# Eight pieces instead of one or two for a table sent to HBM, and three waits moved by some columns, in a one-core 512-token kernel

## What is computed

```python
def chunk(xc):                                   # 128 tokens
    s = ...                                      # scores of 8 heads against 2 x 128 sub-keys
    top_s, top_i = lax.top_k(s, PEER_TOPK)
    cand_s = top_s[:, :, 0, :, None] + top_s[:, :, 1, None, :]
    cand_i = top_i[:, :, 0, :, None] * PEER_N_KEYS + top_i[:, :, 1, None, :]
    ...
    best_s, best_pos = lax.top_k(cand_s, PEER_TOPK)
    idx = jnp.take_along_axis(cand_i, best_pos, axis=-1)
    g = jax.nn.softmax(best_s, axis=-1)
    u = jnp.take(expert_u, idx, axis=0)
    v = jnp.take(expert_v, idx, axis=0)
    act = jax.nn.gelu(jnp.einsum('td,thkd->thk', xc, u))
    return jnp.einsum('thk,thkd->td', (g * act).astype(v.dtype), v)
```

## Time and profile before

| | before |
|---|---|
| median of 3 runs | 3500.95 us (3498.36 to 3501.43) |
| profiled execution | 3489.53 us, its span 3487.6 us |
| mean granted TensorE clock | 0.959 |
| TensorE busy | 3200.6 us, 92% of the span |
| VectorE / ScalarE / GpSimd busy | 1991.2 / 1329.8 / 1312.2 us |
| moved by DMA | 636.86 MB, mean 183 GB/s |

### The profile page before, as it was taken

The page is one execution under the profiler, slowest core; times in us unless marked ns, Lnnn a source line. Parts: engine busy times, 40 slices in busy tenths (PEclk is TensorE's granted clock), DMA queues, the critical chain, the costliest instruction groups (busy, mean ns, idle before and its releaser), DMA issues.

```text
span 3487.6 us, 44563 instructions
## 1 busy us (share of the span) xinstructions
PE 3200.6 (92%) x15088; PEld 2733.2 (78%) x15088; DVE 1991.2 (57%) x2967; ACT 1329.8 (38%) x1959; POOL 1312.2 (38%) x654
## 2 busy tenths in 40 slices
PE   4999779998999989999968778999989897999999
PEld 3888658886888778788856657899979897888887
DVE  6552375512553154411047676878768675788887
ACT  3222232223322232322234553244849482333333
POOL 3444334443444444344423203365433333222321
PEclk9999879999999999999989889999999898999999
DMA  5554325532554222222312103254798989999997
GB/s 225 193 192 145 102 89 194 193 109 73 201 194 141 97 79 97 87 97 98 99 52 69 49 19 103 91 167 155 241 340 252 339 290 386 321 367 359 364 361 275
DMA packets 234647, 636.86 MB, mean 183 GB/s; under 512 B 22560, under 2 KB 104736, under 8 KB 233504
## 3 DMA queue, kind: packets, MB, share of 16 engines
q1 hardware_dynamic: 87408, 318.49, 26.8%
q10 hardware_dynamic: 110256, 182.59, 14.7%
q0 software_dynamic: 36864, 134.23, 10.7%
HBM read 580.69 MB, written 54.53 MB: 182 GB/s over the span
## 4 chain that ended last, share of the span: by engine, by line
issue 39%; PE 36%; POOL 17%; DMA 4%; DVE 3%; ACT 1%; POOLq 0%; ACTq 0%; DVEq 0%
POOL wlo L473 17%; PE bank L1854 5%; PE bank L1856 5%; PE bank L1855 5%; PE bank L1524 5%; PE bank L1525 5%; PE bank L1526 5%; DMA ring<-u_rows_dram,cell_u 4%; PE bank L1815 3%; DVE ring L1373 1%; PE bank L1721 1%; POOL ring L492 0%; DVE wlo L1361 0%; DVE rstd L966 0%; DVE sp L1279 0%
## 5 line engine op out<-in xcount | busy, mean ns | idle before, releaser
L473 POOL TENSOR_TENSOR wlo<-raw,whi 128x1024 fp32r<-128x1024 f32 x394 | 999.7, 2539 | 1458.2 <-ACT whi L511 1457.9
L1524 PE MATMUL bank<-hhi,whi 128*128 128x512 f32 (+1 forms) x2832 | 1062.4, 375 | 60.2 <-DVE wlo L1361 28.8
L1525 PE MATMUL bank<-hlo,whi 128*128 128x512 f32 (+1 forms) x2832 | 1052.6, 372 | 0.0
L1526 PE MATMUL bank<-hhi,wlo 128*128 128x512 f32 (+1 forms) x2832 | 1052.3, 372 | 0.0
L511 ACT ACTIVATE whi<-raw 128x1024 fp32r<-128x1024 f32 x599 | 633.7, 1059 | 1010.4 <-PE bank L1526 618.3
L1524 PEld LDWEIGHTS bank<-hhi,whi 128*128 128x128 f32 x2832 | 537.7, 190 | 136.3 <-DVE wlo L1361 29.7
L1525 PEld LDWEIGHTS bank<-hlo,whi 128*128 128x128 f32 x2832 | 537.3, 190 | 71.6 <-issue 1.4
L1526 PEld LDWEIGHTS bank<-hhi,wlo 128*128 128x128 f32 x2832 | 536.4, 189 | 71.8
L927 DVE CUSTOM_DVE_ANT_0 ada_raw<-ada_raw,cond_row 128x1024 f32<-128x1024 f32 x128 | 307.5, 2433 | 152.0 <-DMA ada_raw<-ada_dram 152.0
L1361 DVE TENSOR_TENSOR wlo<-raw,whi 128x1024 fp32r<-128x1024 f32 x205 | 250.7, 1223 | 115.5 <-ACT whi L511 93.0
L1854 PE MATMUL bank<-whi,we 128*128 128x512 f32 x768 | 299.8, 390 | 14.6 <-ACT act_out L804 14.6
(11 more groups left out here) (244 smaller groups left out, 3682.2 us busy)
## 6 DMA issues: line engine op xcount, KB each, us to landing
raw<-stream_dram SPq DMA_DIRECT2D x599, 512.0 KB
ada_raw<-ada_dram ACTq DMA_DIRECT2D x128, 512.0 KB, 4.0
expert_acts<-act_out ACTq DMA_DIRECT2D x128, 192.0 KB
g_ring<-expert_weights ACTq DMA_DIRECT2D x128, 192.0 KB
act_in<-expert_acts ACTq DMA_DIRECT2D x128, 192.0 KB
first_raw<-ada_dram ACTq DMA_DIRECT2D x8, 1024.0 KB, 23.2
expert_weights<-spread ACTq DMA_DIRECT2D x2, 4096.0 KB, 25.0
x<-xin_dram SPq DMA_DIRECT2D x1, 2048.0 KB, 12.0
```

The costliest lines, as they stand in the source:

```text
L473: pool.tensor_tensor(wlo[:, s, :, :], raw[:, s, :, :], whi[:, s, :, :].bitcast(F32), ALU.subtract).then_inc(lo_ready, 1)
L1524: pe.matmul(bank, whi[:, s, b, :], rhi, start=start, stop=False)
L1525: pe.matmul(bank, whi[:, s, b, :], rlo, start=False, stop=False)
L1526: return pe.matmul(bank, wlo[:, s, b, :], rhi, start=False, stop=stop)
```

## The change

The table of each tile goes out in 8 pieces of 16 rows (1.05 MB) each, one ahead of each of the first 8 gap columns; the gap's columns are unrolled where a loop stood. The exponentials of a tile move from behind the 12th column of its lead to behind the 8th. `x_back` moves ahead of the 9th column of the last gap, and waits for the first half of the last tile's pieces, whose space it takes. ScalarE no longer waits for the table before the first loads of the down stage (the wait at `x_back` covers the rows that these read). TensorE's wait for the last gelu moves from before row 0 of the down stage to before its second pair of banks, 6 matmuls later.

```diff
-EARLY = NK // 2
+PIECE = 16
+PIECES = NK // PIECE
...
             for tt in range(TT):
-                columns_run(LEAD_AT[tt], LEADS[tt])
+                columns_run(LEAD_AT[tt], LEADS[tt] - 4)
                 act.wait_ge(below_ready, tt + 1)
                 act.activation(expo[:, :, :], below[:, :, :], ACT.Exp).then_inc(exp_ready, 1)
+                columns_run(LEAD_AT[tt + 1] - 4, 4)
             for j in range(DT):
                 if j:
-                    act.wait_ge(spilled, 16 * j)
+                    act.wait_ge(spilled, 16 * PIECES * j)
...
-                if j < DT - 1:
-                    act.dma_start(expert_weights[j], spread[:, :, :]).then_inc(spilled, 16)
-                    columns_run(CHUNK_AT[j] + CHUNKS, GAPS[j])
-                else:
-                    act.dma_start(expert_weights[j][:, 0:EARLY, :], spread[:, 0:EARLY, :]).then_inc(spilled, 16)
-                    act.dma_start(expert_weights[j][:, EARLY:NK, :], spread[:, EARLY:NK, :]).then_inc(spilled_late, 16)
+                for k in range(GAPS[j] - 4 * (j == DT - 1)):
+                    if k < PIECES:
+                        rows = slice(PIECE * k, PIECE * k + PIECE)
+                        act.dma_start(expert_weights[j][:, rows, :], spread[:, rows, :]).then_inc(
+                            spilled if j < DT - 1 or k < PIECES // 2 else spilled_late, 16)
+                    elif k == PIECES:
+                        act.wait_ge(spilled, 16 * PIECES * (DT - 1) + 16 * PIECES // 2)
+                        act.dma_start(x_back[:, :, :], x_kept).then_inc(x_landed, 16)
+                    column(CHUNK_AT[j] + CHUNKS + k, None)
...
-            columns_run(NK - GAPS[-1], GAPS[-1] - 4)
-            act.wait_ge(spilled, 16 * DT)
...
-            act.dma_start(x_back[:, :, :], x_kept).then_inc(x_landed, 16)
...
-            act.wait_ge(spilled_late, 16)
+            act.wait_ge(spilled_late, 16 * PIECES // 2)
...
                 for tt in range(1, TT):
+                    if m == 0 and tt == 2:
+                        pe.wait_ge(gelu_done, NK)
...
-            pe.wait_ge(gelu_done, NK)
```

## The result

The changed kernel takes **3480.15 us** (median of 8 runs, 3472.88 to 3486.08), beside 3497.99 us (3487.12 to 3504.87) for the kernel before in the same series: ratio 0.9949, 95% interval [0.9934, 0.9964]. Against the 3500.95 us of the first runs that is 3483 us; the forecast was 3482. The profiled execution takes 3476.22 us, with a span of 3474.4 us, so 13.3 us less than the profiled one of before.

The account below looks back on a forecast made before the run. TensorE's own work and the volume the DMA engines move were taken as the bounds, with waits for `chosen` in the leads. Terms -14 - 4 + 0 - 1 = -19 us took 3500.95 to 3482 us, range 3446 to 3504.

Parts of the forecast that it names:

- The exponentials, -14: In the leads: exponentials four columns earlier let TensorE find `chosen` ready, -14 us, bounds 10.2 and 14.5.
- 10.2 us of waiting: In the leads: TensorE's three waits of 3.4 us for `chosen` would go, 10.2 us.
- the half microsecond given back: In the leads: the first weighted one-hot table is late next, so 0.5 us of the gain is returned.
- the 4.3 us for the clock: In the leads: time at reduced clock after the waits would go, 2.5 us and 1.8 us.
- The pieces in the two gaps, -4: First two gaps: pieces let queues end more evenly while volume sets the length, -2 us each, -4 in all.
- the first idle time: First two gaps: TensorE's idle time for `wlo`, 21.0 us in total, should go because 8 KB packets share fairly.
- The last gap, 0: Last gap: pieces and `x_back` ahead only move bytes within a saturated stretch, 0 us, bounds -5 and +5.
- TensorE's wait, -1: Start of down stage: six half-clock matmuls fall into the idle time, -1 us, bounds 0 and -2.5.
- Order was the limit after all: Gaps: DMA rate hides waste, first idle times go and the second doesn't grow, 38 us, 3448 us; chance 0.20.
- The gaps give back what the leads win: Gaps: refilled slots cost +2.3 us each, gathers ahead of down-stage loads +5, total 3496 us; chance 0.12.
- ScalarE's queue becomes the slow one: Gaps: q10 gets only 151 GB/s, +13 us in each, ScalarE stands at `spilled`, 3525 us; chance 0.10.
- Short rows far apart write slowly: Table writes: 8 KB runs 64 KB apart at half rate, 20.6 us more per table, 3548 us; chance 0.03.

Follow-up runs that it names:

- the last pair of experiments: Changed kernel with 12 of the two gaps' 28 gathers moved into the leads: pieces one a column 3475.53 us, all eight issued together 3462.68 us.

## Why the prediction was right, and where it was not

**The exponentials, -14: right, by its own steps.** 309.71 to 295.52 us is -14.2; the exponentials alone give -14.2, and taking them out of the changed kernel returns 15.8. The terms hold one by one: 10.2 us of waiting became 0.5, the half microsecond given back, and the 4.3 us for the clock are 4.5 us less of busy time, with both stretches of the earlier trace rows at 1.00. Ratio 0.9957 is 15 us of the whole.

**The pieces in the two gaps, -4: wrong in sign, and the step can be named.** The prediction said that the first idle time goes, that the second grows by nearly as much, and that the volume sets the end. The first two are there (21.0 us of waits for `wlo` gone, 13.8 grown to 42.0). The third is half of the matter: volume moves the end (4.19 MB more cost 9.4 and 13.6 us), but so does the order of issue, by 13.9 us at the same volume to be moved. The idle time grew by 7.2 us in the two gaps, and TensorE's busy time fell by 6.1, one restart at half clock less in each, so the length stayed. What failed is "Pieces leave fewer moments in which one queue's long packets end unevenly, so I take a gain". I looked for what pieces do to a packet's turn and not for when the last one is issued. In the kernel before the table had landed 27.1 us after its issue, and `weigh` waited for VectorE; the landing had 25 us to spare. One a column puts the eighth piece 29.8 us behind the first, and it needs another 25.5 us, while the other queues fill the time with bytes that nobody waits for. That is more than was to spare. `weigh` moved from 52.7 to 55.4 us after the first issue, and what it waits for is the table now, not VectorE. Four kernels with a piece a column and 28 gathers in the gaps took 301.8 to 302.6 us for the two; the three with tables issued at once 297.8, 298.6 and 301.6 (the kernel before). So the price is up to 4 us here; it is 13.9 us with twelve gathers fewer. The two ends of the wait tell why. Issued at once or as one transfer, VectorE's one-hot table is what ends it, 50.7 to 52.6 us after the first issue with 28 gathers in the gaps and 42.3 to 44.3 with 16. Issued one a column, the landing ends it, after 52.3 to 55.3 and 48.2 us: fewer gathers bring VectorE forward by some 8 us, and the landing only by 4 to 7.

**The last gap, 0, and TensorE's wait, -1.** `x_back` is worth nothing that can be told (618.28 and 618.77 us), as forecast. TensorE's wait is -1 by the sum and not seen (618.42 with it in the old place, 618.77 in the new). TensorE starts on the down stage 84.1 us after the last table's first issue instead of 89.3, runs the six matmuls at half clock as forecast, and then waits 3.3 us more for the last gelu, until 90.3 us. The gelu came 1 us later, which takes the forecast microsecond back. Idle once in this gap, as the text had it, TensorE is not: its waits for `wlo` there are 8.4 us, as before (7.7).

**The rivals.** *Order was the limit after all* fell: no gap of the changed kernel is shorter by 5 us, and the rate up to `weigh` is 398 GB/s. Yet it was nearer than I gave it credit for, since in the last pair of experiments the order of issue alone is worth 13.9 us. *The gaps give back what the leads win*: its cause is there, 22.01 MB ahead of `weigh` (21.5 were its figure) instead of 20.48, at a size of 1 us. *ScalarE's queue becomes the slow one*: its point of decision, 189 GB/s for q10, was passed: 9.98 MB in 55.4 us are 180 GB/s, and ScalarE stands at `spilled` for 34.0 us in the two gaps. That is the cause at work here, to which I gave 0.10. Its price was 2.7 us of `weigh` in the first gap and not 13, for the queue got 180 GB/s and not 151. *Short rows far apart write slowly* fell: the pieces' rows lie 64 KB apart, and with all eight issued together the stretch to `weigh` has 393 GB/s. The Trainium skill ("DMA: Bandwidth & Descriptors", section Latency and other measured facts) has its half rate, 103 GB/s instead of 214, for rows 4 MiB apart, and still 207 for rows 512 KiB apart; no run here has rows so far apart. Nor did transfers of 1 MB cost rate here: with pieces issued at once and with single transfers the DMA moved 393 and 390 GB/s up to `weigh` in the runs with twelve gathers. The 341 and 425 GB/s of that page of the Trainium skill (section Bandwidth) are for loads; the tables are writes, beside two busy queues.

The forecast of 3482 us owes something to luck: -14 came true, -4 was +1, and the spread between one profile and the median (13.3 and 17.8 us of gain) is as large as the rest. The stretches of the two profiles add up to 12.6 us of gain, where the sum of the prediction has 19.

## What to carry to other kernels

Where the DMA is full, ask of each transfer that somebody waits for when its last byte lands: cutting it and issuing the parts one by one lets more past, and it arrives later at the same rate. Whether that costs anything depends on what else the waiting engine needs, and how late that is. An instruction for which another engine waits 13 us is worth as much as all of that, and costs one line to move. And moving work out of a full stretch pays only into an engine's idle time: four dots where VectorE waited for TensorE won, eight spread over its selection lost in the leads nearly what the gaps gave.

## What the runs showed of the hardware

VectorE's product `gain`, 128x128, which follows the exponentials of the first tile, took much longer in the changed kernel. Before and after:

```profile
2300.38 0.29 DVE L1423 TENSOR_TENSOR gain<-expo,esum 128x128 f32<-128x128 f32 x1
```

```profile
2292.95 1.95 DVE L1425 TENSOR_TENSOR gain<-expo,esum 128x128 f32<-128x128 f32 x1
```

Before, GpSimd was idle at that moment, from 2297.4 to 2302.2 us. After, it was in a row of four subtractions, whose timeline row is

```profile
2284.73 12.43 POOL L474 TENSOR_TENSOR wlo<-raw,whi 128x1024 fp32r<-128x1024 f32 x4 [3.76 <-ACT whi L512]
```

A dot of 1.22 us took 6.31 us in the run with twelve gathers and whole tables, beside an issue of a gather and two subtractions on GpSimd (VectorE's timeline, then GpSimd's):

```profile
2390.09 6.31 DVE L1382 CUSTOM_DVE_ANT_0 ring<-ring,h_row 128x1024 f32<-128x1024 f32 x1
```

```profile
2389.59 0.95 POOL L494 DMA_INDIRECT ring<-u_rows_dram,cell_u  x1
2390.56 4.75 POOL L475 TENSOR_TENSOR wlo<-raw,whi 128x1024 fp32r<-128x1024 f32 x2
```

The subtractions end at 2395.31 us and the dot at 2396.40, 1.1 us behind them, nearly its usual length: it looks as if it ran only when they were done. The same dot took 6.31 to 6.34 us in all four kernels with twelve gathers moved. Not every operation is lengthened, so what decides it is not shown here; that VectorE can be held up beside GpSimd's work is what the rows say, and it is why a tile of VectorE's work can't be costed from the durations of a stretch in which GpSimd rests.
